# Experts ranked into five sizes of share, with a 96 and a 32 on one item's column tiles

## The reference, cut to what matters

```
for e in range(N_EXPERTS):                                   # 64
    h = jax.nn.silu(t @ w_gate[e]) * (t @ w_up[e])           # (512,1024) @ (1024,256), twice
    out = out + gates[:, e:e + 1] * (h @ w_down[e])          # (512,256) @ (256,1024)
```

## Time and profile before

| | us |
|---|---|
| median of 3 runs | 1225.75 (1224.99 to 1227.96) |
| the profiled execution | 1224.93 |
| its span in the profile | 1222.8 |
| first gate and up product of the expert phase, to last output row copied | 544.49 to 1151.27 |

### The profile page before, as it was taken

One profiled execution on the slowest core, in us unless ns is written; L12 is line 12 of the kernel. 1 busy time (PEld: TensorE's weight loads), 2 busy tenths in 40 slices (PEclk: granted clock), 3 DMA queues, 4 the chain that ended last, 5 costly groups with the idle time before them and its releaser, 6 DMA issues.

```text
span 1222.8 us, 11833 instructions
## 1 busy us (share of the span) xinstructions
PE 1084.4 (89%) x3631; PEld 522.5 (43%) x3631; DVE 443.2 (36%) x1018; ACT 175.3 (14%) x429; POOL 364.5 (30%) x488
## 2 busy tenths in 40 slices
PE   5999999988978887819999999999899899999676
PEld 3444845455556553304434443343333333343232
DVE  0402337637262456732332233222222212222137
ACT  1100113224121120001111111111111101111300
POOL 1100000000000011746554554555444345445200
PEclk9999996899999998969999999999999999999989
DMA  8600035000006142117899998999999999999293
GB/s 310 246 1 0 1 150 204 1 1 1 1 2 250 76 152 106 36 24 275 323 347 357 374 377 339 412 413 413 413 406 410 388 384 408 407 379 394 99 442 120
DMA packets 60385, 288.58 MB, mean 236 GB/s; under 512 B 17492, under 2 KB 18572, under 8 KB 34496
## 3 DMA queue, kind: packets, MB, share of 16 engines
q1 hardware_dynamic: 38096, 251.15, 51.4%
q0 software_dynamic: 20016, 35.80, 8.0%
q10 hardware_dynamic: 2240, 1.22, 0.4%
HBM read 279.61 MB, written 32.05 MB: 255 GB/s over the span
## 4 chain that ended last, share of the span: by engine, by line
PE 66%; DMA 17%; DVE 10%; issue 5%; ACT 1%; SPq 1%; POOL 1%; POOLq 0%; DVEq 0%; ACTq 0%
PE bank L1656 23%; PE bank L1361 23%; DMA expert_slots<-in_exp_w_up 15%; PE bank L1631 9%; PE bank L1516 4%; PE bank L1366 4%; PE bank L1470 1%; DMA residual<-in_x 1%; DMA expert_slots<-y_rows 1%; DVE ln_stats L1060 1%; DVE weights L1261 1%; DVE max_sum L1002 1%; PE bank L1454 1%; SPq L440 1%; DVE residual L1074 1%
## 5 line engine op out<-in xcount | busy, mean ns | idle before, releaser
L1656 PE MATMUL bank<-expert_slots,proj 128*128 128x512 f32 (+1 forms) x1088 | 388.9, 614 | 47.7 <-issue 25.1
L1656 PEld LDWEIGHTS bank<-expert_slots,proj 128*128 128x128 f32 (+1 forms) x1088 | 149.2, 171 | 257.7 <-issue 248.5
L675 POOL DMA_INDIRECT proj<-h_rows,idx_col x224 | 227.0, 1013 | 97.8 <-issue 54.4
L1631 PE MATMUL bank<-expert_slots,proj 128*128 128x512 f32 (+1 forms) x544 | 194.5, 598 | 0.0
L616 POOL TENSOR_TENSOR rsqrt_io<-rsqrt_io,minus_half 128x1 f32<-128x1 f32 (+2 forms) x20 | 17.2, 861 | 480.0 <-DVE rsqrt_io L1064 249.9
L1361 PE MATMUL bank<-expert_slots,act_transposed 128*128 128x512 f32 (+2 forms) x344 | 142.5, 572 | 0.0
L1121 DVE TENSOR_TENSOR proj<-proj,bank 128x256 f32<-128x256 f32 x57 | 24.0, 421 | 280.9 <-ACT proj L811 280.7
L1268 DVE STREAM_TRANSPOSE proj<-proj 128x1024 f32<-128x1024 f32 x54 | 109.4, 2025 | 23.8 <-DMA proj<-h_rows,idx_col 23.6
L1631 PEld LDWEIGHTS bank<-expert_slots,proj 128*128 128x128 f32 (+1 forms) x544 | 71.3, 166 | 107.1 <-issue 107.1
L1361 PEld LDWEIGHTS bank<-expert_slots,act_transposed 128*128 128x128 f32 x344 | 65.0, 190 | 71.8 <-issue 71.2
L1276 DVE COPY weights<-bank 128x512 f32<-128x512 f32 x53 | 36.7, 692 | 150.6 <-PE bank L1631 150.6
(11 more groups left out here) (238 smaller groups left out, 819.4 us busy)
## 6 DMA issues: line engine op xcount, KB each, us to landing
expert_slots<-in_exp_w_gate SPq DMA_DIRECT2D x64, 1024.0 KB, 10.7
expert_slots<-in_exp_w_up SPq DMA_DIRECT2D x64, 1024.0 KB, 20.4
expert_slots<-in_exp_w_down SPq DMA_DIRECT2D x64, 1024.0 KB, 23.6
expert_slots<-y_rows SPq DMA_DIRECT2D x4, 4096.0 KB, 19.0
expert_slots<-in_w_in SPq DMA_DIRECT2D x3, 2048.0 KB, 20.3
weights<-in_w_o SPq DMA_DIRECT2D x1, 4096.0 KB, 13.4
proj<-h_rows,idx_col POOLq DMA_INDIRECT x224, 6.3
residual<-in_x SPq DMA_DIRECT2D x4, 512.0 KB, 14.5
```

Source lines behind the costliest of these rows:

```text
L675: pool.indirect_dma_start(out=XG[p][:, g * 256:(g + 1) * 256], out_offset=None, in_=h2_rows.rearrange("t (q d) -> (t q) d", q=4), in_offse ...
L1631: last = nc.tensor.matmul(y_banks(b)[i][r, :], HT[b % 2][:, c, r], SLOTS[w][1][:, c, i * 512:(i + 1) * 512], start=(c == 0), stop=(c == 1))
L1656: last = nc.tensor.matmul(banks[b % 2][r, :], XGT[RING[b]][:, c, r], SLOTS[w][0][:, :, c, :], start=(c == 0), stop=(c == NC - 1))
```

## The change

The ranked experts get five sizes of share: ranks 0 to 3 256 places, 4 to 21 128, 22 to 29 96, 30 to 51 64, and 52 to 59 32. A 96 and a 32 share an item: rows 0 to 63 and 64 to 95 are products with the one expert's weights, rows 96 to 127 with the other's (`three_and_one`), so each product of such an item is three, on 64, 32 and 32 columns. The turns come in four rounds of nine items: a long turn (four items as before), a split turn (two such shared items on four slots), and a plain turn (three items, as the short turns were); three plain turns follow. That is 4 + 4 x 9 + 3 x 3 = 49 items. All 64 experts still are fetched once, four in a turn, 16 turns. The sizes stated above fit: rank 22 has 67 tokens for 96 places and rank 52 has 25 for 32, so there are no extra items.

The lists are laid out in item order, and GpSimd reads its rows from them directly; the tables `gather_at` and `scatter_at` go away. `item_counts` gains steps for the new sizes.

```
+def three_and_one(a, b):
+    return (slice(0, 64), a), (slice(64, 96), a), (slice(96, P), b)
+def halves(a, b):
+    return (slice(0, 64), a), (slice(64, P), b)
+ROUND_ITEMS = [(0, whole(0)), (0, whole(0)), (0, whole(1)), (0, halves(2, 3)),
+               (1, three_and_one(0, 1)), (1, three_and_one(2, 3)),
+               (2, whole(0)), (2, whole(1)), (2, halves(2, 3))]
+LAST_ITEMS = [(0, whole(0)), (0, whole(1)), (0, halves(2, 3))]
+RANKS = [(4, 8, 4 * 4, [(36, 4), (0, 1)]), (4, 4, 4 * 6, [(36, 4), (0, 1)]),
...
+         (4, 4, 0, [(4, 4), (0, 1)])]
@@ SP: the fetches, one stretch of items at a time
+            def stretch(s, items, turn):
+                turns = [turn_no for turn_no, _ in items]
+                e = None
+                freed = []
+                for b, (turn_no, parts) in enumerate(items):
+                    if b == 0 or turns[b - 1] != turn_no:
+                        e = [expert(turn(turn_no), w) for w in range(4)]
+                    more = b + 1 < len(items) and items[b + 1] == items[b]
+                    ours = [] if more else [(w, e[w]) for w in sorted({w for _, w in parts})]
+                    if ours:
+                        gate_up_done(s + b)
+                    for w, no in ours:
+                        gate_up_weights(sp, w, no)
+                    if freed:
+                        rows_done(s + (b - 1))
+                    for w, no in freed:
+                        down_weights(sp, w, no)
+                    freed = ours
+                rows_done(s + (len(items) - 1))
+                for w, no in freed:
+                    down_weights(sp, w, no)
...
@@ VectorE: the tables
-            step(dve.memset(gather_at[:, :, :], 4 * SEQ * TOP_K))
-            step(dve.memset(scatter_at[:, :], NO_TOKEN))
             step(dve.tensor_scalar(lists[:, :, :], lists[:, :, :], 1, 0xFFFFFFFC, ...))
-            def places_of(k0, k1, b0, b1, col):
...
-            places_of(LONG, TURNS, 2, 3, SMALL_COL + HUGE)
+            dve.tensor_scalar(lists[:, :, :], lists[:, :, :], quarter[:, 0:1], None, ALU.add).then_inc(lists_ready, 1)
@@ TensorE: the gate and up products of item b
                     for half in range(2):
                         for c in range(4 * half, 4 * half + 4):
                             for r, w in parts[b]:
-                                last = nc.tensor.matmul(banks[b % 2][r, :], XGT[RING[b]][:, c, r], SLOTS[w][0][:, :, c, :],
+                                last = nc.tensor.matmul(banks[b % 2][r, :], XGT[at(b)][:, c, r], SLOTS[w][0][:, :, c, :],
                                                         start=(c == 0), stop=(c == NC - 1))
```

More of the change, by code:

```diff
@@ L417, in y_banks, with round_start, last_start, lag @@
             return banks[2 + 2 * (b % 2):4 + 2 * (b % 2)]
[L423 to L433, removed]
+        def round_start(k):
+            return k * N_ROUND + FIRST
+        def last_start(k):
+            return k * N_LAST + LAST_ITEM0
+        def lag(b):
+            return 1 if b == 0 else 2
+        def ring(b):
+            return (FIRST + b) % 3
+        def round_uses(k, b):
+            return k * (N_ROUND // 3) + (FIRST + b) // 3
+        def last_uses(k, b):
+            return k * (N_LAST // 3) + (LAST_ITEM0 + b) // 3
+        def first_uses(k, b):
+            return b // 3
         block = ctx.enter_context(nc.Block())
@@ L514, in rows_done @@
                 sp.wait_ge(down_done, s + (NT + 1))
[L516 to L539, removed]
@@ L559, in _ @@
+            stretch(0, FIRST_ITEMS, lambda i: 0)
+            with sp.Fori(0, ROUNDS) as k:
+                stretch(round_start(k), ROUND_ITEMS, lambda i: k * ROUND_TURNS + (ROUND0 + i))
+            with sp.Fori(0, n_short) as k:
+                stretch(last_start(k), LAST_ITEMS, lambda i: k + LAST0)
             sp.wait_ge(y_all, 1)
@@ L630, in _ @@
                                     base=0, pattern=[[-1, N_EXP]], channel_multiplier=1))
[L631 to L638, removed]
+            r = 0
+            for n, places, first, ((step0, n0), (step1, n1)) in RANKS:
+                step(pool.iota(iota_i[:, r:r + n].rearrange("p (k i) -> p k i", i=n1), pattern=[[step0, n0], [step1, n1]],
+                               base=first, channel_multiplier=0))
+                step(pool.memset(cap_tab[:, r:r + n], float(places)))
+                r += n
+            step(pool.tensor_copy(base_tab[:, :], iota_i[:, 0:N_EXP]))
             pool.nop().then_inc(tables_ready, 1)
@@ L1249, in item_counts @@
[L1249 to L1254, removed]
+                two = lambda r, n: by_rank[:, r:r + n].rearrange("p (k b) -> p k b", b=2)
@@ new lines, in item_counts @@
+                rounds = fetch_i[:, 0:LAST0 - 1, :].rearrange("p (k j) b -> p j k b", j=ROUND_TURNS)
+                full, split, plain = (rounds[:, j, :, :] for j in range(ROUND_TURNS))
+                last = fetch_i[:, LAST0 - 1:LAST0 - 1 + LAST_TURNS, :]
+                extra = fetch_i[:, LAST0 - 1 + LAST_TURNS:TURNS - 1, :]
+                extras = owner[:, 0:MAX_EXTRA].rearrange("p (k b) -> p k b", b=3)
+                step(dve.tensor_copy(full[:, :, 0], by_rank[:, 0:4]))
+                step(dve.tensor_copy(full[:, :, 1], by_rank[:, 4:8]))
@@ new lines, in item_counts @@
+                step(dve.tensor_copy(plain[:, :, 0:2], two(8, 8)))
+                step(dve.tensor_copy(last[:, :, 0:2], two(16, 6)))
+                step(dve.tensor_copy(split[:, :, 0], two(22, 8)[:, :, 0]))
+                step(dve.tensor_copy(split[:, :, 2], two(22, 8)[:, :, 1]))
+                step(dve.tensor_copy(full[:, :, 2:4], two(30, 8)))
+                step(dve.tensor_copy(plain[:, :, 2:4], two(38, 8)))
+                step(dve.tensor_copy(last[:, :, 2:4], two(46, 6)))
+                step(dve.tensor_copy(split[:, :, 1], two(52, 8)[:, :, 0]))
@@ L1255, in item_counts @@
+                step(dve.tensor_copy(split[:, :, 3], two(52, 8)[:, :, 1]))
+                step(dve.tensor_copy(extra[:, :, 0:3], extras))
+                step(dve.tensor_copy(extra[:, :, 3], extras[:, :, 2]))
                 dve.nop().then_inc(counts_ready, 1)
@@ L1332, in _ @@
-            turn(0, 4)
-            with dve.Fori(1, LONG) as k:
-                turn(k, 4)
-            with dve.Fori(LONG, n_short + LONG) as k:
-                turn(k, 3)
+                    xg_transpose(s + (b + 1), at(b + 1), uses(k, b + 1) + 1)
+                    hidden(s + (b + NT), b, lag(b))
+                    if b:
+                        y_copy(s, b - 1, at(b - 1), uses(k, b - 1))
+                y_copy(s, n - 1, at(n - 1), uses(k, n - 1))
+            stretch(0, 0, FIRST, lambda b: b % 3, first_uses)
@@ L1337, in _ @@
+            with dve.Fori(0, ROUNDS) as k:
+                stretch(round_start(k), k, N_ROUND, ring, round_uses)
+            with dve.Fori(0, n_short) as k:
+                stretch(last_start(k), k, N_LAST, ring, last_uses)
             dve.wait_ge(y_act, 1)
@@ L1633, in rows_half, with stretch, slots @@
                 return last
-            def turn(k, parts):
-                n = len(parts)
-                s = turn_start(k, n)
+            def stretch(s, items, turn, at):
+                n = len(items)
+                parts = [p for _, p in items]
+                def slots(b):
+                    return sorted({w for _, w in parts[b]})
                 def rows_free(b):
-                    for _, w in parts[b]:
-                        pe.wait_ge(down_in[w], (k + 1) * 16)
-                    free = 1 if isinstance(s, int) and b < 2 else s + (b + 2 - lag(n, b))
+                    for w in slots(b):
+                        pe.wait_ge(down_in[w], (turn(items[b][0]) + 1) * 16)
+                    free = 1 if isinstance(s, int) and b < 2 else s + (b + 2 - lag(b))
                     pe.wait_ge(y_act, free)
@@ L1648, in turn @@
                 for b in range(n):
-                    for _, w in parts[b]:
-                        pe.wait_ge(gate_up_in[w], (k + 1) * 32)
+                    for w in slots(b):
+                        pe.wait_ge(gate_up_in[w], (turn(items[b][0]) + 1) * 32)
                     pe.wait_ge(xt_dve, s + (b + 1))
-                    pe.wait_ge(h_ready, s + (b + NT + 1 - lag(n, b)))
+                    pe.wait_ge(h_ready, s + (b + NT + 1 - lag(b)))
                     for half in range(2):
```

180 lines of the change are left out of this document (68 added, 112 removed).

## The result

Four runs of the changed kernel have a median of 1256.24 us (1252.77 to 1258.65), four of the kernel before 1226.74. The ratio is 1.0238, with an interval of 1.0215 to 1.0261: 29.5 us slower. The forecast was 1264, that is 37 us slower. The profiled execution's span is 1252.2 us against 1222.8, 29.4 more.

The account below looks back on a forecast made before the run. It took TensorE, 89% busy, and in the short turns weight fetches at a DMA share of 0.99 as the bound. Phase 649.4 - 606.8 = +42.6, list -4.4, together +38.2 us: 1263.1, as median 1264; range 1202 to 1285.

Parts of the forecast that it names:

- the rival case on the faster side: Expert phase: tiles of different widths overlap and the DMA sets the pace; 1206 us, between 1191 and 1221; chance 34%.
- the mechanism that the forecast took: Shared items' products: same-width tiles run together, but each change of width empties the array; 2.07 us a block.
- The shared item: Split turn of two 96-and-32 items: between 23.2 us with all tiles overlapping and 72 with none; 51 taken.
- The middle case: Shared items: same-width tiles overlap, changes of width empty the array; item 25.5 us, split turn 51, total 1264; chance 53%.
- The 1.05 us: Extra time per turn around one halves item, put down to six changes of width, about 0.175 us each.
- Fewer items: Expert phase: without waits 576.0 us before, 538.1 after if shared items cost no more than halves items; 38 less.
- The sum without waits: Expert phase before the change: first turn 44.24 us, four long turns of 43.17, eleven short of 32.64; 576.0 in all.
- The waits: Expert phase: TensorE's 30.8 us of waiting, nearly all for weights, go; a round needs 126.8 us of TensorE, 109 of DMA.
- The lists: Before the first item: without the old tables GpSimd starts 4.4 us earlier, all on the path; added `item_counts` steps cost nothing.
- The sum: Whole kernel: phase +42.6 us and list -4.4, together +38.2 on the profiled execution, 1263.1; median 1264.
- The rival that widths mix freely: Shared items: different widths run at once, split turn 23.2 us; DMA gains 15 us, the list 19 in all; 1206; chance 34%.

Follow-up runs that it names:

- one-width kernel: The changed kernel with a shared item's 96 rows cut into three tiles of 32 columns instead of a 64 and a 32: 1210.24 us, ratio 0.9867 to the kernel before.

## Why the prediction held, point by point

The range, 1202 to 1285, takes in most of the rival case on the faster side as well, so the time alone says little. What held is the mechanism that the forecast took, and each sign that it named: two shared items of 51 us rather than 23 (48.5), loads in clusters 1 us apart, a DMA share under 0.9 (0.89 from 540 to 1181), the first item at about 540.

- **The shared item.** The middle case was the right one: tiles of one width together, and at each change the next weights loaded only when the products of the other width are over. It rested on one row, the change from 128 to 64 columns; that 64 to 32 behaves alike was a guess that came true. The split turn was put at 51 us and is 48.5. A change of width inside an item is not 0.175 us but (1.99 - 1.72) / 2, 0.13 to 0.14. The 1.05 us from which 0.175 was worked out is not changes alone: the two transposes between 64-column products take 0.43 us to the next start (620.33 to 620.76 in the kernel before), where they take 0.23 among whole ones. And there are 21 changes inside an item, where 24 were counted. Over four rounds that is 4 x 2.5 = 10 us less than forecast; the first turn (0.8), the last three (0.4) and the list (0.6) came out dearer, and about 8 of the 10 are left, the gap between the 38.2 forecast and the 30.1 measured.
- **Fewer items.** The sum without waits (44.24, 43.17 and 32.64 us for the turns) came within a microsecond where the trace shows it: first turn 45.04, last three 98.26 against 97.9. The first turn has no wait; its first 24 instructions take 13.40 us instead of 12.58, and its granted clock is 0.94 instead of 0.95. The long turn was not read by itself. The prediction takes 578.20 in the earlier trace rows for the start of the third item; it is the second half of the fourth item's gate and up products, and the 10.53 us from item to item stands.
- **The waits.** All 30.8 us of the kernel before but 0.2 are gone, as forecast, because TensorE's 124.3 us a round exceed the DMA's 109.
- **The lists.** 4.4 us forecast, 3.76 in the first item's start. VectorE, whose added steps of `item_counts` were put at nothing, still waited for the list, which arrived at 530.4 instead of 529.8 (timeline of VectorE):

```profile
530.40 0.34 DVE L1324 TENSOR_SCALAR mem_k_v<-mem_k_v 128x340 uint32<-128x340 uint32 x1 [5.38 <-DMA mem_k_v<-token_list]
```

- **The sum.** Phase +42.6 forecast, 640.7 - 606.8 = +33.9 measured; start -4.4 and -3.8; together +38.2 and +30.1, and the span says +29.4.
- **The rival that widths mix freely** is refuted by the first trace. Its price came out: it gave 1206, and the two kernels that stand for it, with four tiles or with two, measure 1210 and 1209. In part that was luck. Of the 30 us that the DMA could have gained if it never paused, the prediction took half without a row to say why half; the phase got 12.5 us shorter, and the changed order of turns then won another 10.

## What to carry to other kernels

For float32 products of 128 x 512, the only ones tried, column tiles of 64 and of 32 did not run at once, and tiles of one width did: cut a 96 into three 32s rather than a 64 and a 32, even at the price of more instructions. Whether it holds for other types or sizes no run shows. And once the bytes bound a phase, fewer items stop paying; what pays then is to look for the place where the DMA idles and to free a buffer sooner there, here one window with a DMA share of 0.77. But the order has to be tried: one that freed a slot sooner in another turn was 13 us slower.

## What the runs showed that I had not expected

Halving the down fetches gave 36 us where 10 to 25 were expected. The expectation went by 1188 us for a phase of 538, and that sum was wrong, as said above: it would be about 1154. 30 MiB, 31.5 MB, are 79 us at 400 GB/s, more than the one-width kernel's waits (594.3 - 554.7 = 39.6 us in its window), so the bytes were no bound any more. Yet the phase came down to 560.1 us only. TensorE is busy for 545.4 of it and still waits for down matrices in four places, 12.7 us in all: some waiting is left even where the DMA has time to spare. Four 32-column tiles each load and multiply in the time of one 128-column product (3.64 against 3.60 us for the same four blocks). And one chip reached the expert phase 12 us later than another (first item of the same kernel at 554.51 and 541.93), with the time from there to the last item's start 567.3 and 570.5 us, so ratios to a kernel of the same chip were needed.
